# Weight tiles split on GpSimd in two pieces of 512 columns instead of four of 256

## What is computed

```python
h = rms_norm(x, norm_w) * (1 + scale) + shift
proj = h @ w_in                      # 1024 -> xBC (2048), z, dt, u, v, z_g, gates
y_m = ssd_branch(...)                # depthwise conv, chunked scans both ways
y_g = u * spatial_mix(layer_norm(gelu(v))) * silu(z_g)
merged = sigmoid(gl_m) * (y_m @ w_out_m) + sigmoid(gl_g) * (y_g @ w_out_g)
x = x + gate * (merged @ w_out)
```

## Time and profile before

| what | value |
|---|---|
| median of three runs | 1401.28 us |
| the profiled execution, its own time | 1401.26 us |
| its span, first to last instruction | 1399.5 us |
| TensorE busy | 1387.0 us, 99% of the span |
| VectorE busy | 1027.1 us, 73% |
| GpSimd busy | 1029.1 us, 74% |
| ScalarE busy | 467.1 us, 33% |
| mean granted TensorE clock | 0.999 of full |

### The profile page before, as it was taken

One profiled execution on the slowest core, in us unless ns is written; L12 is line 12 of the kernel. 1 busy time (PEld: TensorE's weight loads), 2 busy tenths in 40 slices (PEclk: granted clock), 3 DMA queues, 4 the chain that ended last, 5 costly groups with the idle time before them and its releaser, 6 DMA issues.

```text
span 1399.5 us, 27040 instructions
## 1 busy us (share of the span) xinstructions
PE 1387.0 (99%) x10101; PEld 1331.1 (95%) x10101; DVE 1027.1 (73%) x1503; ACT 467.1 (33%) x1039; POOL 1029.1 (74%) x1421
## 2 busy tenths in 40 slices
PE   8999999999999999999999999999999999999997
PEld 5899999999999999999998999999999999999997
DVE  6988679665677688999978766976566776869234
ACT  5432123214766333001252323241266661320122
POOL 3789886696554499998869898657765546979763
PEclk9999999999999999999999999999999999999999
DMA  9362665123766555444334455722346665453222
GB/s 366 126 151 76 191 167 159 61 66 127 188 179 192 177 204 212 150 151 155 106 136 122 107 165 149 192 86 61 106 135 191 193 173 201 139 190 120 76 76 91
DMA packets 198047, 206.85 MB, mean 148 GB/s; under 512 B 76592, under 2 KB 163760, under 8 KB 196784
## 3 DMA queue, kind: packets, MB, share of 16 engines
q1 hardware_dynamic: 116000, 155.13, 35.6%
q10 hardware_dynamic: 81936, 50.16, 12.4%
HBM read 179.23 MB, written 26.02 MB: 147 GB/s over the span
## 4 chain that ended last, share of the span: by engine, by line
PE 98%; DVE 1%; DMA 0%; SPq 0%; issue 0%; ACT 0%; DVEq 0%; ACTq 0%
PE acc L718 79%; PE X L684 5%; PE acc L684 3%; PE X L972 2%; PE X L952 2%; PE X L988 1%; PE X L1013 1%; PE acc L866 1%; PE X L981 1%; DVE p_lo L1606 1%; DMA ada_pre<-in_wada 0%; DVE ssq L1581 0%; PE X L825 0%; DVE xr L2143 0%; PE X L910 0%; PE acc L732 0%
## 5 line engine op out<-in xcount | busy, mean ns | idle before, releaser
L617 POOL CAST w_hi<-w_st 128x256 fp32r<-128x256 f32 x696 | 410.5, 604 | 337.1 <-PE acc L718 162.2
L621 POOL TENSOR_TENSOR w_lo<-w_st,w_hi 128x256 fp32r<-128x256 f32 x696 | 645.0, 936 | 0.0
L718 PE MATMUL acc<-h_hi,w_hi 128*128 128x320 f32 x1696 | 402.1, 318 | 0.0
L718 PE MATMUL acc<-h_lo,w_hi 128*128 128x320 f32 x1696 | 386.3, 309 | 0.0
L718 PE MATMUL acc<-h_hi,w_lo 128*128 128x320 f32 x1696 | 386.2, 309 | 0.0
L718 PEld LDWEIGHTS acc<-h_hi,w_hi 128*128 128x128 f32 x1696 | 284.4, 188 | 14.7 <-issue 11.8
L718 PEld LDWEIGHTS acc<-h_hi,w_lo 128*128 128x128 f32 x1696 | 283.5, 188 | 0.0
L718 PEld LDWEIGHTS acc<-h_lo,w_hi 128*128 128x128 f32 x1696 | 283.4, 188 | 0.0
L1824 DVE SCALAR_TENSOR_TENSOR cv<-raw,convw_sb,cv 128x642 f32<-128x642 f32 x128 | 137.2, 1072 | 4.5
L1540 DVE SCALAR_TENSOR_TENSOR ada_acc<-ada_st,sc,ada_acc 128x512 f32<-128x512 f32 x112 | 107.8, 1002 | 1.8
L1280 ACT ACTIVATE cvt<-cv 128x642 f32<-128x642 f32 x32 | 23.8, 744 | 158.1 <-DVE cv L1824 158.1
(11 more groups left out here) (264 smaller groups left out, 2322.5 us busy)
## 6 DMA issues: line engine op xcount, KB each, us to landing
w_st<-in_wts SPq DMA_DIRECT2D x174, 512.0 KB, 3.7
cum_bc<-cum_dram ACTq DMA_DIRECT2D x80, 256.0 KB, 5.0
ada_st<-in_wada SPq DMA_DIRECT2D x34, 512.0 KB, 4.3
ex_bc<-ex_dram ACTq DMA_DIRECT2D x64, 128.0 KB, 3.1
ada_pre<-in_wada SPq DMA_DIRECT2D x14, 512.0 KB, 8.9
xs<-xs_dram SPq DMA_DIRECT2D x64, 80.0 KB, 3.8
mga_dram<-c_buf SPq DMA_DIRECT2D x16, 320.0 KB, 5.2
xf<-xf_dram SPq DMA_DIRECT2D x4, 1280.0 KB, 7.1
```

The source lines that it names most:

```text
L617: nc.gpsimd.tensor_copy(quarter(w_hi, slot, q), quarter(w_st, slot, q)).then_inc(s_pool, 1)
L621: nc.gpsimd.tensor_tensor(quarter(w_lo, slot, q), quarter(w_st, slot, q), f(quarter(w_hi, slot, q)), ALU.subtract).then_inc(w_split, 1)
L718: last = mm(a[:, hf, 0:n1], w[:, s, cols], x[:, k, hf * HALF:hf * HALF + n1], start=(k == 0 and n == 0), stop=(k == KC - 1 and n == 2))
```

## The change

GpSimd makes two pieces of each tile from the third on. Half 0 is columns 0 to 255 and 512 to 767 (chunks 0, 1, 4, 5), half 1 the rest. `w_split` grows by two per tile, so all targets are counted with `split_base`. TensorE waits in an ordinary tile for the half that holds its chunk, and in a v tile for both halves before the first matmul. SP waits for the same event as before.

```diff
-WQ = 4
+WQ = 2
+WB = KC // 2 // WQ
...
+def split_base(t):
+    return 2 * KC // 2 + WQ * (t - 2)
...
-            sp.wait_ge(w_split, WQ * (t - 1))
+            sp.wait_ge(w_split, split_base(t - 1))
...
-        def quarter(w, slot, q):
-            return w[:, slot, :].rearrange("p (b q n) -> p q b n", b=2, n=P)[:, q, :, :]
+        def half_of(w, slot, q):
+            return w[:, slot, :].rearrange("p (b q n) -> p q b n", b=2, n=WB * P)[:, q, :, :]
...
-                    split_lo(slot, q, 2 * WQ * i + (base + WQ * slot + q + 1))
+                    split_lo(slot, q, 2 * WQ * i + (base + KC - 2 * WQ + WQ * slot + q + 1))
...
-                pe.wait_ge(w_split, WQ * t + 3 + i)
+                pe.wait_ge(w_split, split_base(t) + WQ)
...
-            pe.wait_ge(w_split, WQ * t + k % WQ + 1 if t > 1 else FIRST_SPLIT[t][k // 2])
+            pe.wait_ge(w_split, split_base(t) + k % (KC // 2) // WB + 1 if t > 1 else FIRST_SPLIT[t][k // 2])
```

More of the change, by code:

```diff
@@ L616, in split_hi @@
         def split_hi(slot, q):
-            nc.gpsimd.tensor_copy(quarter(w_hi, slot, q), quarter(w_st, slot, q)).then_inc(s_pool, 1)
+            nc.gpsimd.tensor_copy(half_of(w_hi, slot, q), half_of(w_st, slot, q)).then_inc(s_pool, 1)
         def split_lo(slot, q, n):
             pool.wait_ge(s_pool, n)
-            nc.gpsimd.tensor_tensor(quarter(w_lo, slot, q), quarter(w_st, slot, q), f(quarter(w_hi, slot, q)),
+            nc.gpsimd.tensor_tensor(half_of(w_lo, slot, q), half_of(w_st, slot, q), f(half_of(w_hi, slot, q)),
                                     ALU.subtract).then_inc(w_split, 1)
```

## The result

The changed kernel takes 1426.05 us (five runs, 1424.33 to 1426.39) against 1401.26 us (five runs, 1400.85 to 1401.42): 24.8 us or 1.74% slower, the ratio 1.0174 with a 95% interval of 1.0163 to 1.0185. The forecast was no change that can be told, 1402.2 us. The profiled execution took 1426.39 us, its span is 1424.6 us.

The account below looks back on a forecast made before the run. TensorE, busy 1387.0 of 1399.5 us, was taken as the bound. v tiles 0.1, position 58 0.4 and 0.25 in the second layer, VectorE 0.2 made +0.95 us on 1401.26: 1402.2 us, range 1401.0 to 1404.6.

Parts of the forecast that it names:

- 6.2 us at worst: Split of a v tile by GpSimd: 3.8 us undisturbed plus four disturbances of 0.6 us from VectorE.
- position 58: Tile whose weights land late: TensorE's first chunk 0.4 us late (0 to 0.9), in the second layer 0.25 (0 to 0.7).
- the one on VectorE: VectorE beside long subtractions waits up to 1.34 us instead of 0.7, then catches up; charged 0.2 us in all.
- the thin place that I worked out: Evacuation at 342.56 ends at 343.37, TensorE wants the bank at 344.00: 0.6 us of room.
- VectorE becomes late: Rival: six thin places all miss by 0.3 to 0.6 us, longer chains behind; +2 to +4 us, chance 0.09.
- six thin places: Places in both layers where TensorE closely follows VectorE, with 0.3 to 1.1 us of room; at most 0.6 us each.
- The first rival: v tiles: disturbed split stays 7.4 us, so waits of 4.3 to 6.8 us come, plus 0.65; about 1407, chance 0.09.

## Why the prediction was wrong

**What held.** TensorE had no wait to give back. The cast at 512 columns takes 0.60 us and the subtraction 1.27 undisturbed (0.68 and 1.34 were taken); the estimate of 1.28 us from the Trainium skill (GPSIMD Engine Reference, section 3.1) was nearer. GpSimd's busy time fell to 806 us (below 950 was the mark). Splits of v tiles took 3.9 to 5.7 us, under the 6.2 us at worst, and no v tile was late. At position 58 the wait is 0.33 us with 0.5 us of lag, against 0.4 forecast; the second layer's has 0.5 against 0.25.

```profile
501.57 0.53 PE L724 MATMUL acc<-h_hi,w_hi 128*128 128x320 f32 x2 [0.33 <-POOL w_lo L627]
```

**The step that failed** is the one on VectorE: "In sum GpSimd's occupation shrinks (3.8 against 4.2 us a tile), so VectorE falls behind for a moment and catches up while GpSimd idles", charged with 0.2 us. It priced what VectorE loses by GpSimd's total time. The runs show that a conv instruction loses GpSimd's time less 0.36 us at each meeting. Halving the number of pieces took away half of that free time, and what exceeded it grew from 1.5 to 2.3 us a tile. Instead of gaining 0.4 us a tile VectorE lost up to 0.8, and its busy time rose by 93.5 us. Against the term of 0.2 us stand 16.2 us of new waits for VectorE and for what stands behind it, and with the restarts and the clock about 23 of the 25.1 us. The rows for it were at hand: a conv instruction was known to take between 887 and 1254 ns, and to sort those by what GpSimd did beside them would have shown 0.90 against 1.25 us, from which 512 columns follow. I measured only what VectorE does to GpSimd, and took the other direction from GpSimd's durations ("up to 1.34 us instead of 0.7", where 0.92 and 0.36 are measured). Even the 0.6 us I misread as "about one conv instruction": that one takes 0.89 us alone, so this direction has 0.3 us that cost nothing, too. And the thin place that I worked out, the evacuation L1988 at 342.56, can't be held up in this way: its executions take 806 to 822 ns before and 808 to 822 ns now.

**The second error** is the reading "TensorE never waited for it between 60 and 1386 us" as room. No wait says that room isn't negative, not how much there is. In the stretch from 50 to 175 us VectorE was busy for 98.7 of 125 us before, and from 550 to 660 for 99.6 of 110; in the changed kernel it is 109.7 of 128 and, from 560 to 670, 106.7 of 110. The rival "VectorE becomes late" named the mechanism, but gave it +2 to +4 us and a chance of 0.09, from six thin places with an instruction's delay each. The delays of a whole chain add up before they reach TensorE: four conv instructions stand in one chain, `xw` stands behind it in VectorE's order, and the raw evacuation and `v_tok` stand on ScalarE behind `cvt`, which waits for it. And behind three of the waits the clock was down, 4.6 us, which no term had.

**The first rival** (the whole tile is late) was priced at 4.3 to 6.8 us for unchanged split times: by itself it is 4.0 us, with four late tiles instead of seven. In the changed kernel it had no ground: a long instruction was held up no longer than a short one (beside the conv 1.21 us for the cast and 1.87 for the subtraction, 0.6 us over their undisturbed times, as before).

## What to carry to other kernels

Where two engines share a port, price a change of piece size in both directions: sort the partner's instructions by what ran beside them, and take the difference to those that ran alone, form by form, since forms differ in what is free. Cutting work finely costs its fixed part per piece, but each meeting has a part that costs the partner nothing. Of the sizes tried here 256 columns was best: longer subtractions alone lose 8.4 us and longer casts alone 5.2, both together 24.8, and shorter subtractions lose 23.7. Before calling an engine's delay harmless, look at its busy share stage by stage, and at the idle time in the chain that others wait for: a stage at 90% had no room to catch up, and in a stage at 79% a chain of conv instructions still came 2.3 us late, though nobody had waited for it before.

## What the runs showed of the hardware

What a reading GpSimd instruction costs a conv instruction is GpSimd's undisturbed time less a constant, over a factor of eight in columns. From the profiles of the kernels before, changed, one piece, and the two with subtractions of 128 (shortest durations of GpSimd's instructions, medians of the conv instructions beside them, in us; the conv instruction alone takes 0.89):

| GpSimd's instruction | alone | conv instruction beside it | delay | alone less delay |
|---|---|---|---|---|
| subtraction, 128 columns | 0.45 | 0.97 | 0.08 | 0.37 |
| cast, 256 | 0.39 | 0.90 | 0.01 | 0.38 |
| subtraction, 256 | 0.72 | 1.25 | 0.36 | 0.36 |
| cast, 512 | 0.60 | 1.12 | 0.23 | 0.37 |
| subtraction, 512 | 1.27 | 1.80 | 0.91 | 0.36 |
| cast, 1024 | 1.03 | 1.55 | 0.66 | 0.37 |
| subtraction, 1024 | 2.34 | 2.90 | 2.01 | 0.33 |

The constant goes with VectorE's instruction: for the products of L1546 it is about 0.25 us, beside casts and subtractions alike. I had not expected that a cast of 256 columns costs a conv instruction only 0.01 us while it is itself held up by 0.6 us: the two do not pay alike. Nor that three of TensorE's five waits of about 2 us or more behind the opening come with 3.41 us at half clock, so that such a wait costs 1.4 to 1.7 us more than it shows. Length alone doesn't tell which: the two waits for `xw` of 2.2 and 2.5 us in the kernel with long subtractions only have no dip, and the one of 1.9 us in the kernel with long casts only has one.

The Trainium skill (SBUF — State Buffer, Who interferes with whom) says that the second to issue fully blocks until the first is through. The traces agree in that the delay grows one for one with GpSimd's whole duration, but it is smaller by the constant above: not all of the recorded durations is exposed. No run shows in which part of an instruction the free time lies.
